# Mean of squares of the long heads: two reduced-precision products of ones with a high and a low part, in place of one full-precision product

## What is computed

```
s = einsum('bqhid,bkhid->bhiqk', q * ATTN_SCALE, k)
p = softmax(s)
a = p[:, :, 0] - lam * p[:, :, 1]
o = einsum('bhqk,bkhe->bqhe', a, v)
y = o * rsqrt(mean(square(o), axis=-1) + RMS_EPS) * g * (1.0 - lam_init)
```

## Time and profile before

| what | value |
|---|---|
| median of 3 runs | 3313.98 us |
| the profiled execution's own time | 3312.4 us |
| its span, first to last instruction | 3310.8 us |
| PE busy | 3193.8 us (96%) |
| PEld busy | 2610.0 us (79%) |
| DVE busy | 2229.4 us (67%) |
| ACT busy | 1340.8 us (40%) |
| POOL busy | 294.0 us (9%) |
| mean granted TensorE clock | 0.982 |

### The profile page before, as it was taken

One profiled execution on the slowest core, in us unless ns is written; L12 is line 12 of the kernel. 1 busy time (PEld: TensorE's weight loads), 2 busy tenths in 40 slices (PEclk: granted clock), 3 DMA queues, 4 the chain that ended last, 5 costly groups with the idle time before them and its releaser, 6 DMA issues.

```text
span 3310.8 us, 47864 instructions
## 1 busy us (share of the span) xinstructions
PE 3193.8 (96%) x16712; PEld 2610.0 (79%) x16712; DVE 2229.4 (67%) x3528; ACT 1340.8 (40%) x2053; POOL 294.0 (9%) x521
## 2 busy tenths in 40 slices
PE   5899999999999999998999999999998999999997
PEld 0799989788777777788888777777786888888786
DVE  0577778766777765677655777775667899655546
ACT  0445555432444443236522344444325323454424
POOL 0000001101111100110111000000112000000001
PEclk7899999999999999999999999999999999999998
DMA  9765558565444432764755444442563422322233
GB/s 398 248 228 203 205 181 284 190 213 179 158 147 155 156 121 96 252 218 142 260 208 204 147 151 150 137 149 69 182 215 127 142 97 97 101 86 86 102 115 102
DMA packets 111317, 554.45 MB, mean 167 GB/s; under 512 B 17921, under 2 KB 22065, under 8 KB 68305
## 3 DMA queue, kind: packets, MB, share of 16 engines
q1 hardware_dynamic: 51424, 348.15, 29.8%
q0 software_dynamic: 59760, 204.55, 18.3%
HBM read 530.55 MB, written 22.04 MB: 167 GB/s over the span
## 4 chain that ended last, share of the span: by engine, by line
PE 77%; DVE 9%; DMA 4%; issue 4%; ACT 3%; DVEq 2%; ACTq 0%; POOL 0%; SPq 0%; POOLq 0%
PE acc L1260 22%; PE acc L1262 22%; PE acc L1261 22%; PE pv L1384 3%; DMA xy<-in_wm 2%; DVE w_lo L1710 2%; PE S L1358 2%; PE S L1373 1%; DVE gates L1763 1%; DMA gates<-in_wm 1%; ACT w_hi L685 1%; ACT work L685 1%; PE acc L1289 1%; PE acc L1291 1%; PE acc L1290 1%
## 5 line engine op out<-in xcount | busy, mean ns | idle before, releaser
L1260 PE MATMUL acc<-h_hi,w_hi 128*128 128x512 f32 (+1 forms) x4608 | 1676.3, 364 | 11.5 <-DVE w_lo L1710 7.9
L1262 PE MATMUL acc<-h_hi,w_lo 128*128 128x512 f32 (+1 forms) x4608 | 1645.8, 357 | 0.0
L1261 PE MATMUL acc<-h_lo,w_hi 128*128 128x512 f32 (+1 forms) x4608 | 1644.3, 357 | 0.0
L1260 PEld LDWEIGHTS acc<-h_hi,w_hi 128*128 128x128 f32 x4608 | 870.8, 189 | 165.6 <-issue 29.3
L1261 PEld LDWEIGHTS acc<-h_lo,w_hi 128*128 128x128 f32 x4608 | 871.4, 189 | 127.1 <-issue 6.9
L1262 PEld LDWEIGHTS acc<-h_hi,w_lo 128*128 128x128 f32 x4608 | 870.7, 189 | 127.5
L1710 DVE TENSOR_TENSOR w_lo<-raw,w_hi 128x1024 fp32r<-128x1024 f32 x592 | 698.5, 1221 | 207.7 <-ACT w_hi L685 204.6
L685 ACT ACTIVATE w_hi<-raw 128x1024 fp32r<-128x1024 f32 x592 | 593.6, 1053 | 66.1 <-DMA raw<-in_w 36.6
L685 ACT ACTIVATE ev<-acc 128x512 f32<-128x512 f32 (+1 forms) x210 | 110.9, 532 | 834.8 <-PE acc L1262 813.6
L494 POOL DMA_DIRECT2D gates<-in_wm x288 | 153.6, 533 | 1425.8 <-DVE gates L1763 1234.5
L685 ACT ACTIVATE work<-S,small 128x768 f32<-128x768 f32 (+1 forms) x160 | 129.2, 814 | 257.4 <-DVE small L1877 257.4
(11 more groups left out here) (270 smaller groups left out, 2433.5 us busy)
## 6 DMA issues: line engine op xcount, KB each, us to landing
raw<-in_w SPq DMA_DIRECT2D x296, 1024.0 KB, 5.0
gates<-in_wm POOLq DMA_DIRECT2D x288, 512.0 KB, 4.7
xy<-in_wm SPq DMA_DIRECT2D x32, 1024.0 KB, 8.8
x_d<-xy POOLq DMA_DIRECT2D x1, 4096.0 KB, 14.3
qb<-x_d POOLq DMA_DIRECT2D x16, 256.0 KB, 3.8
kb<-x_d POOLq DMA_DIRECT2D x16, 256.0 KB, 4.1
bias_d<-kb POOLq DMA_DIRECT2D x8, 384.0 KB, 20.6
out_y<-xy SPq DMA_DIRECT2D x3, 1024.0 KB, 4.6
```

The source lines that it names most:

```text
L1260: mm(o, w_hi[:, w], h_hi[:, x], start=n == 0, stop=False)
L1261: mm(o, w_hi[:, w], h_lo[:, x], start=False, stop=False)
L1262: last = mm(o, w_lo[:, w], h_hi[:, x], start=False, stop=n == len(ks) - 1)
```

## The change

For the seven heads of pass a and of pass b whose squares lay in t1, ACT now writes the square twice: once in fp32 to t1 and once rounded to fp32r in osq_hi. DVE subtracts the second from the first (osq_lo), between lo and maxima of p = 0. PE multiplies ones, now an fp32r tile, with osq_hi and osq_lo, adding both into misc; it waits for the low part. The two new tiles lie on the last quarter of xy (tiles 12 and 13), which heads don't use. The last head of each pass and all heads of pass c keep the full-precision product. [...]

```diff
+        with nc.sbuf_tensor("xy_front", [P, 12 * SEQ], F32):
+            with nc.sbuf_tensor("osq", [P, 2 * SEQ], F32R) as osq_parts:
+                pass
...
-        ones = sb("ones", P)
+        ones_r = sb("ones", P, F32R)
+        ones = ones_r[:, :].bitcast(F32)
...
+        osq_hi, osq_lo = osq_parts[:, 0:SEQ], osq_parts[:, SEQ:2 * SEQ]
...
# ACT
+                def split_square(i):
+                    act.wait_ge(pv_done, shown(pv_done, At(h0 - 1, 1, i)))
+                    f(t1[:], pv[:, :], ACT.Square)
+                    f(osq_hi, pv[:, :], ACT.Square).then_inc(osq_done, 1)
...
                                 act.wait_ge(qk_ready, shown(qk_ready, At(h0, 1, i)))
-                                squared(i - 1, t1)
+                                split_square(i)
                             value_evac(i - 1)
...
# PE
+                def split_mean_squares(i):
+
+                    pe.wait_ge(osq_lo_done, shown(osq_lo_done, At(7 * PASS[c] - 8, 1, i)))
+                    for x, first in ((osq_hi, True), (osq_lo, False)):
+                        last = mm(misc[:, 0:T], ones_r[:], x, start=first, stop=not first)
+                    last.then_inc(ms_done, 1)
...
                             pe.wait_ge(vt_evac, shown(vt_evac, At(VT0[c], 1, i)))
-                            mean_squares(i - 1, t1)
+                            split_mean_squares(i)
...
# DVE
+                def squares_lo(i):
+
+                    dve.wait_ge(osq_done, shown(osq_done, At(h0 - 1, 1, i)))
+                    tt(osq_lo, t1[:, 0:T], osq_hi.bitcast(F32), ALU.subtract).then_inc(osq_lo_done, 1)
...
                         lo(j_at(phase, i, p) + 1 if proj else j_at(c + "pool", 0, p + 1))
+                        if norm and p == 0:
+                            squares_lo(i)
                         if attn:
                             maxima(i, p)
...
-            nc.vector.memset(ones[:], 1.0)
+            nc.vector.memset(msum[:, 0:1], 1.0)
+            dve.drain()
+            nc.vector.tensor_copy(ones_r[:], msum[:, 0:1].to_broadcast([P, P]))
```

More of the change, by code:

```diff
@@ L260, in build @@
         osq_done = sem("osq_done")
+        osq_lo_done = sem("osq_lo_done")
         ms_done = sem("ms_done")
```

## The result

The changed kernel takes 3318.8 us in the median (3316.9 to 3322.6), the kernel before 3313.6 in the same set of runs (3309.4 to 3316.2). The ratio is 1.0018, 95% interval 1.0011 to 1.0025: 6 us more, with 3.6 to 8.3 as its bounds. The forecast was +6.4. The profiled execution has a span of 3319.1 us; in it the head phases are 6.6 us longer and the rest 1.7 (most of it in the stretch between the two head phases, which in another execution of the same kernel was 2.0 us shorter than before, so it is not the change's).

A forecast was written before the change was run, and what follows sets the result against it. A 58.68 us ring of waits through DVE was taken to bound each head step. Subtract +7.3, less 0.1 and 0.8, gave +6.4 us: 3318.8 from the profiled 3312.4, or 3320.4 from the median 3314.0; range 3313 to 3325.

The forecast's parts named there:

- DVE's ring: Loop of waits from transposes at p = 2 through ACT, DVE and POOL back to them: 58.68 us, the step's period.
- PE could do its part in about 0.2 us less: Head step: PE idles 0.2 to 0.3 us before most p = 2 transposes, read as room below the 58.68 us step.
- The product: PE, p = 1, 14 products: 0.39 us saved each, worth 0 in steps 2 to 7, 0.8 us in step 8.
- The subtract: DVE, between lo and maxima of p = 0: 0.605 us in each of twelve steps, 7.3 us, less 0.1.
- The second square: ACT, before the value evacuation: 0.49 us x 14, hidden, cost 0; done about 1.5 us before DVE comes.
- The sum: Whole kernel: +7.3 - 0.1 - 0.8 = +6.4 us, bounds +5.5 to +9; chance of the forecast 0.70.
- Rival 1: PE sets the pace in the head steps: 14 x 0.39 = 5.5 us faster, 3308.5; chance 0.08.
- Rival 2: DVE's 3.27 us wait for modulation tile 2 swallows the subtract; only step 8's 0.8 us gain remains, 3313.2; chance 0.12.
- Rival 3: DVE's subtract waits for ACT's high part: another 0.5 us a step, +12.4 in all, 3326.4; chance 0.10.
- Rival 4: PE's mean of squares: nothing of the product is cheaper, +7.2 us, inside the forecast's range; no separate chance given.

The follow-up runs named there:

- the product alone: The change without DVE's subtract, PE taking the high part twice; against the kernel before 0.9996, median 0.0 us, step 58.79 / 58.68 us.
- the subtract alone: The change with its product back at full precision, second square and subtract kept; against the kernel before 1.0019, median +6.6 us, step 59.21 / 59.36.
- short-ring kernel: Kernel before with modulation tile 2 moved from p = 0 to between maxima and difference of p = 1; against the kernel before 0.9998, step 58.70 us.
- subtract in the DMA wait: The change with the subtract moved between modulation tiles 1 and 2 of p = 0; against the kernel before 0.9994, step 58.70 / 58.71 us.
- The change again: The unaltered change timed a second time against the kernel before: 1.0016, median +3.8 us, step 59.28 / 59.36 us.
- the 58.31 of the short ring: The change with modulation tile 2 moved to p = 1: step 58.31 us; against the kernel before 0.9984 (subtract moved) or 0.9981 (in place).

## Why the prediction was right, and where it was not

**The bound.** That DVE's ring and not PE's work decides when something is added was right: the transposes of p = 2 stay within 0.06 us of DVE's end in the change, the product alone gives nothing, the subtract alone gives the whole cost. That "PE could do its part in about 0.2 us less" was wrong. It read an idle time of the weight load (PEld) as one of PE; the prediction's own table has PE busy for 58.68 of 58.68 us, and over the whole of pass a's steps (837.68 to 1248.62 us) PE is busy for 410.94 of 410.94. The short-ring kernel shows PE's own step at 58.70 us, and the two kernels in which PE had 0.39 us less to do (product only, subtract in the DMA wait) show the ring at 58.7 (58.68 to 58.79). The two limits are equal to within a tenth of a microsecond; no run shows a reason for it, and it may be chance. An idle time of 0.2 us on a weight load that comes late is not yet a delay: before, the transposes of p = 2 came 13.23 us after those of p = 1 and those of p = 3 again 12.89 us later, without a wait both are 13.07 (rows in the last section). The 0.16 us is caught up. The sum did not suffer from it, because it only used that the ring was not shorter than PE's step; the forecast for the short ring did.

**The product.** 0.39 us each was right to the hundredth (58.70 less 58.31). As forecast it was worth nothing in twelve of the fourteen places. In the last step of each pass it gave 0.54 and 0.44 us rather than 0.39, 1.0 in all for 0.8. The time caught up is in it: the change's last steps (58.15 and 58.13) begin with a wait of 0.86 and 0.85 us and are 0.16 and 0.18 us shorter than the 58.31 of the short ring.

**The subtract.** 0.605 us each was right: the step grew by 0.60 us in pass a and 0.66 in pass b, 7.6 us over twelve steps for the 7.2 of the sum (7.3 less 0.1). The change again (7.0) and the subtract alone (6.6) lie around that number too. The full 0.69 us of an operation that starts only when the one before has drained, which I had weighed with the Trainium skill ("VectorE: DVE Perf Modes", The DRAIN you can't avoid), would give 8.3, more than any of the three; 0.61 from start to start holds here as it did before.

**The second square.** Hidden, with the margin read from the rows (1.5, measured 1.6).

**The sum.** Head phases +6.6 us in the profile (+5.9 in that of the change again), +6 by the ratio, forecast +6.4. The range's lower end of +5.5 doesn't come out of the bounds that the prediction names: 12 x 0.60 less 0.1 and 0.8 is +6.3. The device time told more than the prediction allowed: 0.2% was named as what it can tell, and the interval reached 0.07% to either side.

**The rivals.** Rival 1 was true only once the ring was shortened: it needs some 0.4 us of room, and the kernel had none. The Trainium skill's rule to improve the engine with the highest occupancy ("Perfetto Trace Analysis", Identifying the Most-Contended Engine) judges TensorE, among others, by the busy share of its weight loads. It points at PE here all the same (44.92 us of the step against DVE's 43.39), and an improvement of PE alone gave 0. Rival 2 fell: the wait for tile 2 did not absorb the subtract (3.41 us after 3.33 in the mean), since the fetch starts from DVE's own use of tile 0. Put inside that wait, the subtract is free. Rival 3 fell by its margin. Rival 4 fell with the 58.31 us.

## What to carry to other kernels

An engine that is busy without a gap can be tied with a chain through other engines; before work is moved from it, list for each of its waits by how much the awaited thing was early, and where that is zero every time, follow the chain back round the loop. Work inside such a ring costs its full start-to-start time, the same work in one of the ring's waits costs nothing, and a saving on the tied engine shows only after the ring has been shortened. When two limits are equal, each of the two edits alone measures as nothing or as a loss, and both together as a gain.

## What I had not expected of the hardware

A weight load that waited 0.2 us did not delay the step. Below are the transposes of p = 3, p = 1 and p = 2 in the kernel before, and then the same three in the kernel before on the short ring, where none waits:

```profile
909.41 0.81 PEld L1373 LDWEIGHTS S<-ident,work 128*128 128x128 f32 x6
...
941.97 0.81 PEld L1373 LDWEIGHTS S<-ident,work 128*128 128x128 f32 x6
...
955.20 0.65 PEld L1373 LDWEIGHTS S<-ident,work 128*128 128x128 f32 x6 [0.20 <-DVE work L1888]
```

```profile
909.60 0.81 PEld L1373 LDWEIGHTS S<-ident,work 128*128 128x128 f32 x6
...
942.16 0.81 PEld L1373 LDWEIGHTS S<-ident,work 128*128 128x128 f32 x6
...
955.23 0.81 PEld L1373 LDWEIGHTS S<-ident,work 128*128 128x128 f32 x6
```

The spacing is 13.23 us (p = 1 to 2) and 12.89 (p = 2, at 896.52, to 3) with the wait, 13.07 and 13.07 without. The rows show where the time is caught up: the six loads take 0.64 or 0.65 us behind a wait and 0.81 without one, 0.17 less. In the change the same holds of longer waits: 0.69 and 0.89 us of idle time in the step shown, less some 0.17 each, on top of PE's 58.31 give 59.5. In a step of the kernel with the subtract twice (898.04 to 958.15), 1.26 and 0.85 us give 60.08 for 60.11. In the product-only step shown, 0.69 gives 58.8 for 58.95, so the working is rough to a tenth. So short idle times of the loads overstate what a wait costs by up to 0.2 us each.
